# Forgetting attention, prompt part: when the maximum matmuls of later query blocks are issued

## The chip, the cores and the metric

The kernel is one launch on one core of a Trainium2 chip. It computes one inference step of a hybrid decoder layer. The metric is the device time of the core in microseconds (us), median of several executions. The engines are called PE (TensorE, with PEld for its weight loads), DVE (VectorE), ACT (ScalarE), POOL (GpSimd) and SP (SyncE, which issues DMAs).

## The reference

Only the attention over the prompt matters here: 8 heads of 64 channels, 4096 positions, causal, with a bias of cumulated forget logarithms.

```python
s = jnp.einsum('bqhd,bkhd->bhqk', q, k, preferred_element_type=jnp.float32) * ATTN_SCALE
s = s + (jnp.transpose(fq, (0, 2, 1))[..., :, None] - jnp.transpose(fk, (0, 2, 1))[..., None, :])
mask = k_pos[None, :] <= q_pos[:, None]
s = jnp.where(mask[None, None], s, -jnp.inf)
p = jax.nn.softmax(s, axis=-1)
return jnp.einsum('bhqk,bkhd->bqhd', p.astype(v.dtype), v)
```

The rest of the layer (input projection, pooling mixer, attention over the paged cache for 32 sample tokens, gates, output projection) runs in other phases, before and after this one, and is not touched.

## The kernel before

The phases run one after the other; the change is in `phase_attend`. The queries of a head are cut into 8 blocks of 512, so there are 64 blocks `b`, with row `j` = 0 to 7 inside head `h`. Block `b` of row `j` is worked through in `j + 1` groups of 512 keys (288 groups `n` in all, 36 a head). The last group of each block holds the causal diagonal: it is called diagonal here, the others full. A group is two steps `s` (576 in all), a step is two halves, and a half is a tile of scores of 128 keys by 512 queries.

The softmax needs the maximum of every query before its block begins. It is found ahead of time in units: one unit is the matmul of 128 queries with 512 keys (L997, in the diagonal chunk narrower, 128, 256 or 384 columns, with one more matmul for the mask, L1000) into one of the two PSUM banks of `mx`, and a DVE reduction of that bank to one column (L928). A block of row `j` has 4 * (j + 1) units, 1152 in all. When all units of block `b + 1` are reduced, DVE combines them (L933, L938), PE spreads the result over a row (`spread_shift`, L1008, four matmuls into the same banks), and ACT copies it into `q_one` (L834); scores of block `b + 1` wait for that copy. A unit, a spread and a sum of weights (`total`, L1060) all take the next of the two banks, and PE waits in `bank_free` until the use before the last one has been read: for a unit, until its reduction is done.

The order of PE is written out by hand. For each step: scores of half 0 (L1028, L1029, and in a diagonal group L1032 for the mask), the first `len // 2` units of the step, scores of half 1, the remaining units. After the last step of a block comes the spread for the next block. After the two steps of a group come the matmuls of weights with values of the step before and of this group's first step (`weigh`, L1049), and in the second group of the next block the sums of weights of the previous one (`total`). PE runs in order, so a unit that waits for its bank holds back everything behind it.

How many units stand in which step is set by `units_by` (the number issued up to step `n`). DVE's order follows the same list: the units of a step, then `combine` in the last but one step of a block, `low_q` (L922) in its last, and `low_k` (L916) in step `first_step[b] + 4` of the blocks of rows 3 to 6 of heads 0 to 6 and of rows 1 and 2 of head 0. That step is the first one of the third group, counted from the block's start. `low_k` makes the low parts of the next head's keys, in 1024 columns, from two tiles in SBUF. POOL adds the weights in pairs (L802, L803) in the meantime, ACT computes the exponentials (L852, in diagonal groups L856).

```python
def units_after(n, half):
    units = units_in(n)
    return units[:len(units) // 2] if half == 0 else units[len(units) // 2:]
```

With `units_by` as it is, a step of the kernel before has two units almost everywhere, and 3 in 22 steps of head 0, where the lead over the running block is built up; the last 17 steps have none.

Of the kernel before, what the change touches and what calls it, by code (L numbers as in the profile page):

```python
# [10 lines left out]

# [1 line left out]

# [21 lines left out]
NT = SEQ // TILE  # L37
TT = TILE // P
# [529 lines left out]
def phase_attend(nc, io, keep):  # L568

    NB = H * NT  # L570
# [3 lines left out]
    EARLY = 3 * TT  # L574
# [10 lines left out]
    def row(b):  # L585
        return b % NT

    quad_base = [sum(row(a) + 1 for a in range(b)) for b in range(NB + 1)]
    NQUAD = quad_base[NB]
    NSTEP = 2 * NQUAD  # L590
    block_of = [b for b in range(NB) for _ in range(row(b) + 1)]
    first_step = [2 * quad_base[b] for b in range(NB)]
    last_step = [2 * quad_base[b + 1] - 1 for b in range(NB)]
    unit_base = [TT * quad_base[b] for b in range(NB + 1)]

    units_by = [0] * NSTEP
    for n in reversed(range(NSTEP)):
        b = block_of[n // 2]
        needed = unit_base[min(b + (2 if n >= last_step[b] - 1 else 1), NB)]
        units_by[n] = max(needed, units_by[n + 1] - 3 if n + 1 < NSTEP else 0)  # L600
    out = EARLY
    for n in range(NSTEP):
        out = units_by[n] = min(max(out + 2, units_by[n]), unit_base[NB])

    def units_in(n):
        return range(units_by[n - 1] if n else EARLY, units_by[n])
# [1413 lines left out]
def build(nc, io):  # L2020
    with ExitStack() as ctx:
        m = Alloc(nc, ctx, "keep")
        keep = {
            "ident": m.sb("ident", [P, P]),
            "ones": m.sb("ones", [P, P]),
            "hs_high": m.sb("hs_high", [P, KC, NS], F32R),
            "hs_low": m.sb("hs_low", [P, KC, NS], F32R),
            "f_tot": m.sb("f_tot", [H, NT]),
        }
        phase_project(nc, io, keep)  # L2030
        phase_decode(nc, io, keep)
        phase_attend(nc, io, keep)
        keep["mix_s"] = m.sb("mix_s", [NS, D])
        phase_gates(nc, io, keep)
        phase_merge(nc, io, keep)
# [34 lines left out]
```

## Time and profile before

| what | us |
| --- | --- |
| median of 3 runs | 3806.81 |
| lowest, highest | 3802.3, 3811.97 |
| profiled execution | 3809.71 |
| its span | 3808.1 |
| prompt attention, first scores to last weigh, in that execution | 1179.4 to 2722.5 |

The profile is of one execution. Times in the rows are counted from the start of its span. "Idle" in brackets is the time that the engine stood still before an instruction, and the name behind the arrow is what ended it. PE rows show a matmul from its start to its modelled end; the next may start before that, so starts are what to compare. The granted clock is a share: 1.00 is 2.4 GHz, 0.50 is 1.2 GHz, and a value between is a mean over a stretch.

### The profile page before, as it was taken

To read this page: it belongs to the slowest core of one execution; us is meant where nothing else is said; L and a number is where in the kernel's file an instruction comes from. 1 tells how busy PE (TensorE), PEld (TensorE's weight loads), DVE (VectorE), ACT (ScalarE), POOL (GpSimd) and SP (SyncE) were. 2 spreads that over 40 slices of the span, in tenths; PEclk is the share of its full clock that TensorE was granted. 3 is DMA by queue.
4 is the path that set the end of the run, shared out by engine and by line. 5 is a ranking of instruction groups with operands and counts; after the bars stand their busy time and mean duration, and the time that the engine had idled before them with its cause. 6 is when DMAs were issued, how large, how long until landed. Compare 5 with 4: busy or idle time off the path is not lost. (4 is left out here: it accounts for less than half of the span.)

```text
span 3808.1 us, 52765 instructions
## 1 busy us (share of the span) xinstructions
PE 3488.4 (92%) x18932; PEld 2413.4 (63%) x18932; DVE 1710.7 (45%) x2708; ACT 1174.9 (31%) x1611; POOL 1196.8 (31%) x1146
## 2 busy tenths in 40 slices
PE   7999999796966999999999999999799999978998
PEld 5777777672814555656565656565367777757887
DVE  3222221251516556555655555555244353445554
ACT  4221221040314445454545454554410000000110
POOL 0000000133333566666666666666500000000000
PEclk9999999796977999999999999999899999989999
DMA  4222332399884121212121212100212111136765
GB/s 147 96 93 102 119 110 78 137 353 353 295 323 99 25 45 34 45 34 45 34 45 34 46 34 45 34 17 12 85 54 77 44 44 55 55 101 186 207 212 163
DMA packets 215996, 392.36 MB, mean 103 GB/s; under 512 B 60135, under 2 KB 102120, under 8 KB 213775
## 3 DMA queue, kind: packets, MB, share of 16 engines
q1 hardware_dynamic: 195079, 322.22, 27.2%
q0 software_dynamic: 20768, 68.17, 4.8%
q8 instruction: 92, 1.51, 0.2%
q14 instruction: 57, 0.47, 0.0%
HBM read 288.50 MB, written 101.99 MB: 103 GB/s over the span
## 5 line engine op out<-in xcount | busy, mean ns | idle before, releaser
L928 DVE TENSOR_REDUCE at_max_parts<-at_mx 128x1 f32<-128x512 f32 (+3 forms) x1152 | 731.4, 646 | 498.3 <-PE at_mx L997 428.9
L802 POOL TENSOR_TENSOR at_pair_sum<-at_probs 128x1024 f32<-128x1024 f32 x224 | 532.0, 2375 | 428.5 <-ACT at_probs L852 428.5
L852 ACT ACTIVATE at_probs<-at_st,at_gap 128x1024 f32<-128x1024 f32 x448 | 497.5, 1112 | 526.9 <-PE at_st L1029 525.9
L1049 PE MATMUL at_o_ps<-at_probs,at_v 128*64 128x512 f32 (+3 forms) x2304 | 544.9, 584 | 0.0
L1028 PE MATMUL at_st<-at_q_all,at_k_all 128*128 128x512 f32 (+3 forms) x1152 | 477.4, 414 | 0.0
L997 PE MATMUL at_mx<-at_k_one,at_q_top 67*128 67x512 f32 (+3 forms) x1152 | 454.0, 395 | 8.7 <-DVE at_max_parts L928 5.9
L1029 PE MATMUL at_st<-at_q_one,at_k_one 67*128 67x512 f32 (+3 forms) x1152 | 439.6, 382 | 0.0
L1028 PEld LDWEIGHTS at_st<-at_q_all,at_k_all 128*128 128x128 f32 x1152 | 218.5, 190 | 225.9 <-ACT at_probs L852 108.7
L93 PE MATMUL ga_acc<-ga_h_high,ga_w_high 128*128 128x512 f32 x768 | 312.3, 407 | 22.5 <-DVE ga_h_low L1293 21.0
L94 PE MATMUL ga_acc<-ga_h_low,ga_w_high 128*128 128x512 f32 x768 | 308.7, 402 | 0.0
L95 PE MATMUL ga_acc<-ga_h_high,ga_w_low 128*128 128x512 f32 x768 | 308.4, 402 | 0.0
L803 POOL TENSOR_TENSOR at_quad_sum<-at_pair_sum 128x512 f32<-128x512 f32 x224 | 287.5, 1284 | 17.5
L1049 PEld LDWEIGHTS at_o_ps<-at_probs,at_v 128*64 128x64 f32 x2304 | 146.8, 138 | 209.2 <-issue 159.4
L997 PEld LDWEIGHTS at_mx<-at_k_one,at_q_top 67*128 67x128 f32 x1152 | 220.2, 191 | 64.6 <-DVE at_max_parts L928 17.1
L1029 PEld LDWEIGHTS at_st<-at_q_one,at_k_one 67*128 67x128 f32 x1152 | 221.2, 192 | 30.1
L93 PE MATMUL mg_acc<-mg_w_high,mg_mix_high 128*128 128x512 f32 x512 | 201.5, 394 | 24.1 <-DVE mg_xs L1598 16.9
L93 PE MATMUL pj_acc<-pj_h_high,pj_w_high 128*128 128x512 f32 x512 | 209.9, 410 | 6.3 <-DVE pj_fs L430 6.3
L1522 POOL MEMSET mg_minus_half<- 128x1 f32 x1 | 0.1, 98 | 656.7 <-POOLq L66 656.7
L95 PE MATMUL pj_acc<-pj_h_high,pj_w_low 128*128 128x512 f32 x512 | 206.1, 403 | 0.0
L94 PE MATMUL pj_acc<-pj_h_low,pj_w_high 128*128 128x512 f32 x512 | 205.8, 402 | 0.0
L94 PE MATMUL mg_acc<-mg_w_low,mg_mix_high 128*128 128x512 f32 x512 | 200.7, 392 | 0.0
L95 PE MATMUL mg_acc<-mg_w_high,mg_mix_low 128*128 128x512 f32 x512 | 200.5, 392 | 0.0
(302 smaller groups left out, 4974.5 us busy)
## 6 DMA issues: line engine op xcount, KB each, us to landing
dc_pages<-in_cache_k_dram SPq DMA_DIRECT2D x128, 256.0 KB, 6.0
dc_pages<-in_cache_k_dram POOLq DMA_DIRECT2D x128, 256.0 KB, 5.7
dc_pages<-in_cache_v_dram SPq DMA_DIRECT2D x128, 256.0 KB, 7.1
dc_pages<-in_cache_v_dram POOLq DMA_DIRECT2D x128, 256.0 KB, 5.7
pj_x<-in_x_prompt_dram SPq DMA_DIRECT2D x32, 512.0 KB, 3.7
scratch_h_t<-pj_h_t SPq DMA_DIRECT2D x8, 2048.0 KB, 9.9
at_q_raw<-scratch_q_t SPq DMA_DIRECT2D x128, 128.0 KB, 3.0
at_k_raw<-scratch_k_t SPq DMA_DIRECT2D x64, 256.0 KB, 4.1
```

The lines of the kernel that those rows point to most:

```text
L93: nc.tensor.matmul(out, lhs_high, rhs_high, start=first, stop=False)
L94: nc.tensor.matmul(out, lhs_high, rhs_low, start=False, stop=False)
L95: return nc.tensor.matmul(out, lhs_low, rhs_high, start=False, stop=last)
L802: chain.link(nc.gpsimd.tensor_tensor(pair, first, second, ALU.add))
L803: nc.gpsimd.tensor_tensor(out, pair[:, 0], pair[:, 1], ALU.add).then_inc(summed, 1)
L852: nc.scalar.activation(probs[:, s % RING], st[:, s % 2], ACT.Exp, bias=bias).then_inc(exp_done, 1)
L928: nc.vector.tensor_reduce(max_parts[:, b % AHEAD, t, c:c + 1], mx[:, bank_of["unit", k] % 2, 0:width], AX_X, ALU.max).then_inc(bank_done, 1)
L997: last = nc.tensor.matmul(mx[:, n % 2, 0:width], q_top[0:KR, b % AHEAD, t * P:(t + 1) * P], k_one[h % 2][0:KR, c * TILE:c * TILE + width], ...
L1028: nc.tensor.matmul(out, k_all[h % 2][:, keys], q_all[:, b % AHEAD, at:TILE], start=True, stop=False)
L1029: last = nc.tensor.matmul(out, k_one[h % 2][0:KR, keys], q_one[0:KR, b % 2, at:TILE], start=False, stop=(c < j))
L1049: last = nc.tensor.matmul(o_ps[half * HD:(half + 1) * HD, b % 2, at:TILE], v[:, h % 2, 4 * c + own], probs[:, s % RING, half, at:TILE], st ...
L1522: nc.gpsimd.memset(minus_half[:], -0.5)
```

## The change

Only `units_by` is computed differently: a step of a diagonal group gets at most one unit, a first step of a full group two and a second step three, from the second head on; in head 0 every step may have three. A floating line (`even`, `lead`) spreads them over the blocks so that each block's units are still issued in time. The number of units, their order, the banks and all other instructions stay as they are.

```diff
-    units_by = [0] * NSTEP
-    for n in reversed(range(NSTEP)):
-        b = block_of[n // 2]
-        needed = unit_base[min(b + (2 if n >= last_step[b] - 1 else 1), NB)]
-        units_by[n] = max(needed, units_by[n + 1] - 3 if n + 1 < NSTEP else 0)
-    out = EARLY
+    def on_diagonal(n):
+        return n // 2 + 1 == quad_base[block_of[n // 2] + 1]
+
+    def most_units(n):
+        return 3 if n < 2 * quad_base[NT] else 1 if on_diagonal(n) else 2 + n % 2
+
+    finished_by = [unit_base[min(block_of[n // 2] + (2 if n >= last_step[block_of[n // 2]] - 1 else 1), NB)] for n in range(NSTEP)]
+    needed = list(finished_by)
+    for n in reversed(range(NSTEP - 1)):
+        needed[n] = max(needed[n], needed[n + 1] - most_units(n + 1))
+    per_head = TT * quad_base[NT] - 2 * NT
+    even = list(itertools.accumulate(1 if on_diagonal(n) else per_head / (2 * (quad_base[NT] - NT)) for n in range(NSTEP)))
+    lead = max(f - e for f, e in zip(finished_by, even))
+    units_by, out = [], EARLY
     for n in range(NSTEP):
-        out = units_by[n] = min(max(out + 2, units_by[n]), unit_base[NB])
+        out = max(needed[n], out, min(out + most_units(n), math.floor(lead + even[n] + 0.01), unit_base[NB]))
+        units_by.append(out)
```

Worked through, the two formulas give these counts of groups by the units of their two steps; "with low_k" are those whose first step has a `low_k` behind its units:

| group | before | after |
| --- | --- | --- |
| full, 2 and 2 | 206 | 90 |
| full, 2 and 3 | 6 | 115, of these 25 with low_k |
| full, 3 and 2 | 0 | 6, of these 2 with low_k |
| full, 3 and 3 | 5 | 6, of these 2 with low_k |
| full, none | 7 | 7 |
| diagonal, 2 and 2 | 56 | 0 |
| diagonal, 3 and 2 | 6 | 0 |
| diagonal, 1 and 1 | 0 | 58 |
| diagonal, 3 and 3, or 3 and 1 | 0 | 3 |
| diagonal, others (2 and 0, 1 and 0, none) | 2 | 2 |

In heads 1 to 6 a head then has 8 diagonal groups with 1 and 1, 12 full ones with 2 and 3 that have no `low_k`, 4 with 2 and 3 that have one (the third group of rows 3 to 6; the third unit of row 3's is 128 wide), and 12 with 2 and 2. Head 7 has no `low_k`.

## Rows read from the trace of the kernel before

**Rows 1.** The page: its first lines.
```profile
span 3808.1 us, 52765 instructions
PE 3488.4 (92%) x18932; PEld 2413.4 (63%) x18932; DVE 1710.7 (45%) x2708; ACT 1174.9 (31%) x1611; POOL 1196.8 (31%) x1146
```

**Rows 2.** Waits of the whole run: engine, line, releaser: us in total, times, longest.
```profile
PE at_mx L1008 <- DVE at_max_parts L928: 39.6, 54, 2.0
```

**Rows 3.** By stretch: A:B us, then busy us of PE, PEld, DVE, ACT, POOL, granted clock, DMA share, GB/s. Four full groups.
```profile
1714.37:1719.23 4.86, 4.86 (x22) 2.67 (x20) 2.77 (x4) 2.23 (x2) 3.66 (x3) 1.00 0.00 0
1292.76:1298.20 5.44, 5.36 (x24) 2.85 (x22) 3.36 (x5) 2.23 (x2) 4.30 (x3) 1.00 0.00 0
1709.48:1714.37 4.89, 4.89 (x25) 2.73 (x21) 3.87 (x6) 2.23 (x2) 2.76 (x3) 1.00 0.00 0
1256.48:1263.12 6.64, 5.36 (x26) 2.89 (x22) 4.80 (x7) 2.23 (x2) 4.91 (x4) 1.00 0.25 68
```

**Rows 4.** Timeline, DVE in the full group at 1714.37: start, us, instruction, count, idle.
```profile
1715.39 2.78 DVE L928 TENSOR_REDUCE at_max_parts<-at_mx 128x1 f32<-128x512 f32 x4 [1.25 <-PE at_mx L997]
```

**Rows 5.** The view by source line: ns shortest/median/longest of the reductions and of low_k.
```profile
L928 DVE TENSOR_REDUCE at_max_parts<-at_mx x1152: 280/692/695, 1169.6 to 2685.8; 128x1 f32<-128x512 f32 x168, 128x1 f32<-128x128 f32 x16, 128x1 f32<-128x384 f32 x8
...
L916 DVE TENSOR_TENSOR at_k_all<-at_k_raw,at_k_all x32: 1221/1222/1461, 1168.3 to 2475.3; 64x1024 fp32r<-64x1024 f32 x32
```

**Rows 6.** Timeline, the two units at the end of the group at 1292.76.
```profile
1295.42 0.98 PE L997 MATMUL at_mx<-at_k_one,at_q_top 67*128 67x512 f32 x2
```

**Rows 7.** Timeline, the full group with low_k and five units at 1256.48.
```profile
1257.67 1.29 POOL L803 TENSOR_TENSOR at_quad_sum<-at_pair_sum 128x512 f32<-128x512 f32 x1
...
1258.59 1.46 DVE L916 TENSOR_TENSOR at_k_all<-at_k_raw,at_k_all 64x1024 fp32r<-64x1024 f32 x1
...
1260.08 1.98 DVE L928 TENSOR_REDUCE at_max_parts<-at_mx 128x1 f32<-128x512 f32 x3
...
1260.83 0.50 PE L997 MATMUL at_mx<-at_k_one,at_q_top 67*128 67x512 f32 x1 [1.28 <-DVE at_max_parts L928]
```

**Rows 8.** By stretch, as rows 3: diagonal groups of rows 0, 1, 2, 5, 6; then row 4.
```profile
1776.55:1781.87 5.32, 4.92 (x31) 3.41 (x30) 3.27 (x7) 3.56 (x8) 1.42 (x3) 1.00 0.01 3
1788.29:1793.99 5.70, 5.63 (x42) 3.47 (x38) 3.40 (x8) 2.47 (x5) 3.57 (x5) 1.00 0.49 126
1803.82:1809.63 5.81, 5.33 (x33) 3.38 (x29) 4.27 (x8) 2.47 (x5) 4.45 (x5) 1.00 0.44 121
...
1882.31:1888.47 6.16, 5.27 (x31) 3.28 (x29) 4.12 (x7) 2.48 (x5) 5.35 (x6) 1.00 0.00 0
1918.74:1924.50 5.76, 5.28 (x33) 3.53 (x31) 3.16 (x7) 2.48 (x5) 4.95 (x5) 1.00 0.00 1
...
1468.37:1476.12 7.75, 6.88 (x32) 3.80 (x30) 3.68 (x7) 2.48 (x5) 5.58 (x6) 0.78 0.00 0
```

**Rows 9.** Timeline, the diagonal group at 1882.31 (2 and 2 units, row 5).
```profile
1882.95 0.45 PE L997 MATMUL at_mx<-at_k_one,at_q_top 67*128 67x512 f32 x1
...
1883.23 0.34 PE L1028 MATMUL at_st<-at_q_all,at_k_all 128*128 128x384 f32 x1
...
1883.43 1.39 DVE L928 TENSOR_REDUCE at_max_parts<-at_mx 128x1 f32<-128x512 f32 x2 [2.19 <-PE at_mx L997]
...
1883.64 0.45 PE L997 MATMUL at_mx<-at_k_one,at_q_top 67*128 67x512 f32 x1
...
1886.25 0.42 PE L1008 MATMUL at_mx<-at_ident_r,at_shift_w 128*65 128x128 f32 x4 [0.89 <-DVE at_max_parts L928]
1886.61 0.20 PEld L1049 LDWEIGHTS at_o_ps<-at_probs,at_v 128*64 128x64 f32 x4
```

**Rows 10.** Timeline, the diagonal group at 2683.98, whose last step has no unit.
```profile
2685.09 1.45 DVE L928 TENSOR_REDUCE at_max_parts<-at_mx 128x1 f32<-128x512 f32 x2 [2.18 <-PE at_mx L997]
...
2686.57 0.36 DVE L933 TENSOR_TENSOR at_max_moved<-at_max_parts,at_gap 128x32 f32<-128x32 f32 x1
...
2687.22 0.46 PE L1008 MATMUL at_mx<-at_ident_r,at_shift_w 128*65 128x128 f32 x4 [0.71 <-DVE at_shift_w L938]
```

More of the change, by code:

```diff
@@ L14 @@
+import itertools
+import math
 from contextlib import ExitStack
```

## The prediction, made before the change was run

> **What bounds the kernel now.** I read the page first: PE is busy for 92% of the span, and DVE, ACT and POOL for less than half of it [rows 1]. The change moves matmuls and reductions inside the prompt attention, which is 1543 us of the span, so I left the page for that stretch and cut it into groups, each from the first L1028 of one group to the first of the next. A full group with four units takes 4.86 us and PE is busy through all of it [rows 3]; there PE's own work sets the time. DVE reduces the four units in 2.78 us without a gap between them [rows 4]: one reduction of 512 columns takes 0.69 us, the median [rows 5], and PE brings a new unit just as often (two score matmuls and one unit). So DVE is half idle over the group, but while the units run it has no slack at all, and with two banks a unit can start only when the reduction before the last one has ended. A diagonal group of rows 3, 4, 5 and 7 takes 6.1 us though its scores are narrower, and PE is busy for 5.27 us of it [rows 8]: PE brings units faster than DVE reduces them, and the spread at the end stands still for 0.89 us until a reduction has freed its bank [rows 9]. Over the run that wait is met 54 times and costs 39.6 us of idle PE [rows 2]. That is what the change can take away. What it adds lands in full groups, where PE never waits now.
>
> **The diagonal groups.** Two units leave each of them. The first that is left stands after the second half of the first step. Where two are there now, the second starts 1.33 us into the group (1883.64 less 1882.31), and the one before it holds 0.28 us of that (1883.23 less 1882.95) [rows 9], so the new one starts at 1.05. Its reduction starts 0.48 us later (1882.95 to 1883.43) [rows 9]. What follows is seen in the one group whose last step has no unit: two reductions take 1.45 us there, so the second begins at about 2685.85, the combine starts at 2686.57 and the spread at 2687.22, now released by the combine [rows 10]: 1.37 us from reduction to spread. So the spread starts at 1.05 + 0.48 + 1.37 = 2.90. PE gets to it at about 2.2 (narrow scores and one more unit), so some 0.7 us of idle stays, by another releaser. From spread to weigh it is 0.36 us and from there to the next group 1.86, up to the group's end [rows 8, 9]: 5.12 us. The low_q and the reduction behind the combine lie beside the 1.86 us of weigh and cost nothing; the exponentials too. Against the groups of now [rows 8] this gives, for rows 0 to 7, 0.20, 0.58, 0.69, 1.04, 1.04, 1.04, 0.64 and 1.04: 6.27 us a head, and 43 us for heads 1 to 7 (seven times, less the last group, which has no units at all). Bounds: 0.1 us either way for each of 55 groups, so 37 to 49.
>
> Six of the diagonal groups of heads 1 to 7 take 7.60 to 7.80 us in place of 6.1. One is shown: its mean granted clock is 0.78, so for a part of it PE ran at 1.2 GHz, behind that same wait [rows 8]. With the idle time before the spread cut and fewer narrow matmuls around it, I take these away: 6 times 1.6, 9.6 us. Bounds 0 and 9.6.
>
> **The fifth unit in a full group.** In heads 1 to 7 there are 84 full groups with 2 and 3 units and no low_k. Head 0 already has two of them with full width, and both took 5.44 us; one is shown [rows 3]. Of the extra 0.58 us about 0.23 is the matmul itself; the rest is pacing: the last two units stand one behind the other, the fifth has to wait for the third's reduction, and PE's next work, the weigh, is behind it in order. The pair spans 0.98 us where a single unit spans 0.40 [rows 6]. 84 times 0.58 is 48.7 us. Below, only the matmul would be left, 19 us; above, nothing in the trace is dearer for this shape, and I allow 0.65, 55 us.
>
> **The fifth unit behind low_k.** In 24 groups of heads 1 to 6 the copy of the keys' low parts stands on DVE between the second unit and the third. With four units it is free: 4.89 us, the third row [rows 3], since the fourth unit's bank needs only the second's reduction. With five it is not. The one such group of head 0 with full widths took 6.64 us, the fourth row [rows 3]: low_k from 1258.59 to 1260.05, the third unit's reduction after it, and PE idle for 1.28 us until that has ended, with the fifth unit and the whole weigh behind it [rows 7]. That is 1.75 us over the four-unit group. In row 3 the third unit is 128 wide, its reduction 0.28 in place of 0.69 [rows 5], so 1.34 there. Per head 3 * 1.75 + 1.34 = 6.59, and for six heads 39.5 us. Bounds: the plain price, 0.58 each, 14 us, and 1.29 us more each (below), 70 us.
>
> What shows in low_k's own row is that it isn't always 1.22 us long: 1.46 where POOL's L803 runs beside its start, until 1258.96 [rows 5, 7]. The Trainium skill, "SBUF — State Buffer", under "SBUF: two separate sides", has a rule for this: a DVE operation with two SBUF inputs and a GpSimd one that reads SBUF exclude each other, and the one that comes second blocks for the whole instruction. By that rule low_k would be held by whatever add of POOL it meets; the trace agrees in direction (1.46 against 1.22), but in its own duration it shows 0.24 us, not a whole add. As a mechanism of this kernel it is a rival below.
>
> These groups are also new places where PE stands still for over a microsecond, longer than before the spreads. The group of rows 7 kept its clock at 1.00 [rows 3]. I put 2 or 3 of 24 at 1.6 us each for a lowered clock, 4 us; bounds 0 and 38.
>
> **Head 0.** It gets ten more steps with three units (32 against 22), at 0.58 us some 6 us, and about 2 us more behind its low_k, and loses as much at four diagonal groups that come down to one and one. I take it as zero, within 8 us.
>
> **Sum.** Of the profiled execution, 3809.7: + 48.7 + 39.5 - 43 - 9.6 + 4 + 0 = + 39.6, so 3849.3. The median of the runs shown is 2.9 us under the profiled execution, so 3846 for the median.
>
> **The rivals.**
> First, the clock: PE's waits behind low_k bring it down to 1.2 GHz in half or all of the 24 groups, as it came down in six diagonal groups of now. For it: those six had only about 0.9 us of idle. Against it: those had narrow matmuls around the wait, and the group of rows 7, with 1.28 us, had none of it. 12 to 24 times 1.6 less the 4 above: 3861 to 3880. Chance 0.08.
>
> Second, the lock: in the new rhythm low_k meets POOL's adds at another point and is held for a whole L803 of 1.29 us [rows 7]. 24 times up to 1.29, 31 us more: up to 3877. That is where the page's rule would lead. Against it: full groups get longer, so POOL has more time and its add should end before low_k comes, not after. If so, low_k falls from 1.46 to 1.22, which gives back up to 6 us. Chance 0.06 for over 3868.
>
> Third, low_k falls out of the way (ready so early or so late that the third reduction isn't behind it): the 24 groups cost 0.58 each, the sum falls by 25 us to 3821. For it: only one row carries the price. Against it: DVE's order is written out, low_k always stands before the third unit. Chance 0.10, half of it within 0.3%.
>
> Fourth, not slower: the fifth unit costs its matmul only, because the reduction that it waits for ends in time. Then 108 fifths at 0.23 cost 25 us against 52.6 saved, and the kernel would be at 3779. It decides where the mean price of the 108 falls below 52.6 / 108 = 0.49 us; the rows have 0.58 and 1.75. Against it: four reductions in 2.78 us with no gap [rows 4] leave none for a unit that comes after 0.23. Chance 0.05.
>
> Fifth, the change does nothing that lasts: what diagonal groups give equals what full ones take, because the banks only move the wait. That would need the low_k groups near the plain price and the clock's 9.6 us full; it gives 3800 to 3818. Chance 0.06.
>
> **How the numbers follow.** The forecast, 3825 to 3860 with 3846 as its middle, has 0.65. The range of 8 in 10, 3822 to 3866, adds the near half of the first and the third rival; what lies above (the clock and the lock at full size) and below (fourth and fifth) is left out. A measurement of this kernel can tell about 0.3%, 11 us, from no change. Slower by over that: the forecast, the first two and half of the third rival, and what is left over near them, 0.87. Within it: the other half of the third and most of the fifth, 0.08. Faster: 0.05.
>
> **What would show it.** In the profile after: diagonal groups of one and one unit at 5.0 to 5.2 us, the spread released by the combine (L938) and no longer by L928; full groups of 2 and 3 at 5.4, with PE idle before the second unit of the last pair; the third groups of rows 3 to 6 in heads 1 to 6 at 6.2 to 6.7, with over a microsecond of idle released by L928; heads 1 to 6 each some 6 us longer, head 7 about 1 us. The wait of L997 for L928 takes the place of L1008's. The prediction is wrong if full groups with five units come in under 5.1 us, or if the low_k groups don't stand out.

## The result and the profile after

| | median us | lowest, highest | ratio to before, 95% interval |
| --- | --- | --- | --- |
| kernel before | 3806.24 | 3802.3, 3811.97 | |
| changed kernel | 3871.49 | 3865.56, 3872.18 | 1.0167 [1.0149, 1.0184] |

The changed kernel is slower by 65 us. The forecast was 3846, its range 3822 to 3866. The sign and the mechanism were right, the size was not. The profiled execution took 3872.18 us, 62.5 us more than the one of before, where the forecast had 39.6. The ratios here and below are those of the fast runs made beside each other, without one execution of the kernel before that took 4614.52 us at a lower clock, so they differ by up to 0.1% from the quotient of two medians.

In the changed kernel the line numbers are 11 higher: the unit is L1008, its mask L1011, its reduction L939, low_k L927, the combine L944 and L949, the spread L1019, scores L1039 and L1040, weigh L1060, POOL's adds L813 and L814. The counts and times by group below are of the one profiled execution of each kernel.

The page: every engine has as many instructions as before, and PE's busy time is longer by 42 us all the same (to be held against rows 1).

```profile
span 3870.6 us, 52765 instructions
PE 3530.9 (91%) x18932; PEld 2408.9 (62%) x18932; DVE 1697.4 (44%) x2708; ACT 1174.5 (30%) x1611; POOL 1195.1 (31%) x1146
```

The waits of the changed kernel (engine, line, releaser: us in total, times, longest). The spread hardly waits for a bank any more (0.9 us, where it was 39.6 before [rows 2]) but for the combine, 19.8 us in all, and the units now wait for the reductions:

```profile
PE at_mx L1008 <- DVE at_max_parts L939: 39.7, 32, 1.5
PE at_mx L1019 <- DVE at_shift_w L949: 19.8, 40, 1.2
PE at_mx L1019 <- DVE at_max_parts L939: 0.9, 2, 0.5
```

Stretches of the changed kernel, with the columns of rows 3 (us, busy us of PE, PEld, DVE, ACT, POOL, granted clock, DMA share, GB/s): a plain full group with five units; a five-unit group with low_k whose clock stayed up, and one whose clock fell; diagonal groups of rows 5 and 7; then head 0, and heads 1 to 7.

```profile
1989.47:1994.91 5.44, 5.30 (x24) 3.04 (x23) 3.14 (x5) 2.23 (x2) 3.72 (x3) 1.00 0.00 0
1895.83:1902.56 6.73, 5.37 (x26) 2.86 (x22) 4.87 (x7) 2.23 (x2) 4.79 (x4) 1.00 0.00 0
1866.00:1873.96 7.96, 6.59 (x27) 3.08 (x23) 4.88 (x7) 2.23 (x2) 5.96 (x4) 0.85 0.26 67
1913.08:1918.56 5.48, 4.71 (x28) 2.82 (x26) 3.28 (x5) 2.37 (x5) 5.10 (x5) 1.00 0.02 3
1994.91:1999.76 4.85, 4.72 (x29) 2.83 (x27) 2.17 (x5) 2.37 (x5) 3.96 (x4) 1.00 0.00 0
...
1179.20:1399.10 219.90, 209.34 (x1068) 120.50 (x1066) 124.74 (x206) 104.81 (x131) 123.03 (x86) 0.92 0.14 32
1399.10:2783.00 1383.90, 1326.84 (x7680) 777.23 (x7679) 727.86 (x1217) 691.20 (x877) 871.10 (x617) 0.99 0.15 35
```

The same two stretches, head 0 and heads 1 to 7, of the kernel before:

```profile
1179.40:1393.90 214.50, 203.89 (x1066) 118.75 (x1064) 126.39 (x205) 104.31 (x131) 124.81 (x88) 0.95 0.14 33
1393.90:2722.50 1328.60, 1293.46 (x7681) 780.86 (x7680) 739.38 (x1218) 691.88 (x877) 871.04 (x614) 0.99 0.16 36
```

The rest of the span differs by less than 2 us. Cutting both traces into their 288 groups, each from the first score matmul of one to that of the next, and adding up by kind gives where the time went:

| kind (heads 1 to 7 unless said) | groups | before | after | difference | forecast |
| --- | --- | --- | --- | --- | --- |
| diagonal | 56 | 337.5 | 283.5 | -54.0 | -52.6 |
| full, five units, no low_k | 84 | 404.7 | 451.8 | +47.1 | +48.7 |
| full, five units, low_k | 24 | 118.0 | 176.9 | +58.9 | +43.5 |
| full, others | 88 | 468.4 | 471.7 | +3.3 | 0 |
| head 0 | 36 | 214.5 | 219.9 | +5.4 | 0 |

The third row of the table stands out. In this trace 12 of the 24 groups had a stretch at 1.2 GHz, as the third row of the fence above; the other twelve took 6.46 us (row 3) or 6.72. This is the wait, in the group at 1895.83, with the columns of rows 7: low_k between the second and the third reduction, and PE idle for 1.36 us before the fifth unit, until the third's reduction had ended.

```profile
1896.83 1.39 DVE L939 TENSOR_REDUCE at_max_parts<-at_mx 128x1 f32<-128x512 f32 x2 [0.57 <-PE at_mx L1008]
...
1898.26 1.22 DVE L927 TENSOR_TENSOR at_k_all<-at_k_raw,at_k_all 64x1024 fp32r<-64x1024 f32 x1
...
1899.51 1.98 DVE L939 TENSOR_REDUCE at_max_parts<-at_mx 128x1 f32<-128x512 f32 x3
...
1900.26 0.50 PE L1008 MATMUL at_mx<-at_k_one,at_q_top 67*128 67x512 f32 x1 [1.36 <-DVE at_max_parts L939]
```

### The profile page after: what moved, and what is told of

The parts are those of the page before. It is cut to its first block and busy times, and to the rows that moved or that the text cites. A ratio compares the mean times of both kernels' runs of the same rounds, so it can differ in the third digit from the quotient of the medians.

```text
span 3870.6 us, 52765 instructions
## 1 busy us (share of the span) xinstructions
PE 3530.9 (91%) x18932; PEld 2408.9 (62%) x18932; DVE 1697.4 (44%) x2708; ACT 1174.5 (30%) x1611; POOL 1195.1 (31%) x1146
## 5 line engine op out<-in xcount | busy, mean ns | idle before, releaser
L939 DVE TENSOR_REDUCE at_max_parts<-at_mx 128x1 f32<-128x512 f32 (+3 forms) x1152 | 730.2, 646 | 576.6 <-PE at_mx L1008 401.9
L813 POOL TENSOR_TENSOR at_pair_sum<-at_probs 128x1024 f32<-128x1024 f32 x224 | 530.5, 2368 | 499.8 <-ACT at_probs L863 499.8
L1060 PE MATMUL at_o_ps<-at_probs,at_v 128*64 128x512 f32 (+3 forms) x2304 | 552.5, 591 | 0.0
L1008 PE MATMUL at_mx<-at_k_one,at_q_top 67*128 67x512 f32 (+3 forms) x1152 | 456.4, 400 | 49.6 <-DVE at_max_parts L939 39.7
L1039 PE MATMUL at_st<-at_q_all,at_k_all 128*128 128x512 f32 (+3 forms) x1152 | 485.1, 421 | 0.4
L1040 PE MATMUL at_st<-at_q_one,at_k_one 67*128 67x512 f32 (+3 forms) x1152 | 441.2, 383 | 0.0
L1039 PEld LDWEIGHTS at_st<-at_q_all,at_k_all 128*128 128x128 f32 x1152 | 219.1, 190 | 232.9 <-issue 157.5
L95 PE MATMUL ga_acc<-ga_h_high,ga_w_high 128*128 128x512 f32 x768 | 311.8, 406 | 23.2 <-DVE ga_h_low L1304 21.0
L1008 PEld LDWEIGHTS at_mx<-at_k_one,at_q_top 67*128 67x128 f32 x1152 | 221.4, 192 | 144.2 <-DVE at_max_parts L939 99.6
L814 POOL TENSOR_TENSOR at_quad_sum<-at_pair_sum 128x512 f32<-128x512 f32 x224 | 287.2, 1282 | 17.6
L1060 PEld LDWEIGHTS at_o_ps<-at_probs,at_v 128*64 128x64 f32 x2304 | 148.0, 139 | 207.6 <-issue 167.8
L1040 PEld LDWEIGHTS at_st<-at_q_one,at_k_one 67*128 67x128 f32 x1152 | 222.0, 193 | 24.9
```

The lines of the kernel that those rows point to most:

```text
L95: nc.tensor.matmul(out, lhs_high, rhs_high, start=first, stop=False)
L813: chain.link(nc.gpsimd.tensor_tensor(pair, first, second, ALU.add))
L814: nc.gpsimd.tensor_tensor(out, pair[:, 0], pair[:, 1], ALU.add).then_inc(summed, 1)
L939: nc.vector.tensor_reduce(max_parts[:, b % AHEAD, t, c:c + 1], mx[:, bank_of["unit", k] % 2, 0:width], AX_X, ALU.max).then_inc(bank_done, 1)
L1008: last = nc.tensor.matmul(mx[:, n % 2, 0:width], q_top[0:KR, b % AHEAD, t * P:(t + 1) * P], k_one[h % 2][0:KR, c * TILE:c * TILE + width], ...
L1039: nc.tensor.matmul(out, k_all[h % 2][:, keys], q_all[:, b % AHEAD, at:TILE], start=True, stop=False)
```

## The experiments

Ten kernels. All but the fifth start from the changed one. A fence has the line numbers of its own kernel.

**1. low_k behind the units of its group.**

```diff
-    low_k_at = {s + 1: c for s, (c, part) in round_k_at.items() if part == 1}
+    low_k_at = {s + 2: c for s, (c, part) in round_k_at.items() if part == 1}
```

> The changed kernel with one edit: low_k stands one step later on DVE, behind the third, fourth and fifth unit of the third group and not between the second and the third. Units, PE's order and diagonal groups stay. Theory (the 24 groups of heads 1 to 6 with five units and low_k, 7.37 us on average in the changed kernel, carry both the wait of PE for the third reduction and the clock that falls behind it): they come down to the price of a plain five-unit group, about 5.4 us, 24 * 1.95 = 46 us less, so 3871 - 46 = 3825, and the granted clock stays at 1.00 in nearly all of heads 1 to 6. Rival 1 (the clock falls for another reason, for instance the five-unit groups themselves): only the wait goes, some 28 us, so 3843, and about a dozen dips of the clock stay. Rival 2 (low_k only moves its wait to the next group): 3871, with L997 idle for L939 in the fourth group.

Measured: 3841.74 us, 1.0092 [1.0074, 1.0111] of before. The 24 groups came down from 7.37 to 5.37 us on average and none had a lowered clock, as the theory said; that is 48 us, where 46 were expected. But the next full group of the block took 5.96 us in place of 5.23, and heads 1 to 7 had three dips of the clock at other places (in the diagonal groups behind row 3's low_k), so the whole came to 3842 and not to 3825. The timeline shows why, the second rival by a cause of its own: low_k now runs beside POOL's pair addition.

```profile
1857.31 2.36 POOL L813 TENSOR_TENSOR at_pair_sum<-at_probs 128x1024 f32<-128x1024 f32 x1 [1.65 <-ACT at_probs L863]
...
1857.71 3.04 DVE L927 TENSOR_TENSOR at_k_all<-at_k_raw,at_k_all 64x1024 fp32r<-64x1024 f32 x1
...
1859.75 2.13 POOL L814 TENSOR_TENSOR at_quad_sum<-at_pair_sum 128x512 f32<-128x512 f32 x1
...
1861.53 0.50 PE L1008 MATMUL at_mx<-at_k_one,at_q_top 67*128 67x512 f32 x1 [0.65 <-DVE at_max_parts L939]
```

low_k takes 3.04 us, against 1.22 in the fence above, and POOL's second addition 2.13 against 1.29 [rows 7]. The starts say more: low_k ends 1.08 us after POOL's first addition (1860.75 against 1859.67), and POOL's second addition ends 1.13 us after low_k (1861.88). Each ends as if it had done next to nothing until the other was through.

**2. The same with POOL's additions left out beside low_k.** The groups with low_k are missing from the sums of weights here.

```diff
+                if n + 1 < quad_base[b + 1] and any(x in low_k_at for x in (2 * n, 2 * n + 1)):
+                    chain.link(nc.gpsimd.memset(out, 1.0))
+                    nc.gpsimd.memset(out[:, 0:1], 1.0).then_inc(summed, 1)
+                    return
```

> The changed kernel with low_k one step later, and in the groups with low_k POOL leaves out the two additions of the weights and writes ones, so the sums of weights lack these groups. In the run with low_k late, low_k took 3.08 us in the median where it takes 1.22 alone, and the fourth group of the block, 4.9 us in the changed kernel, took 5.8. Theory (DVE's low_k and POOL's addition of the same time exclude each other at SBUF): low_k is back at 1.22 us and the fourth groups at 4.9 and 5.5, 22 groups times 1 us and a few dips of the clock behind them: 3842 - 22 - 6 = 3814. Rival (low_k is long there for a reason of its own, such as the reductions around it): still 3 us, 3842.

Measured: 3813.0 us, 1.0006 [0.9997, 1.0016]. low_k is back at its own time. First its row in the view by source line (shortest/median/longest in ns) from the first experiment, then from this one, where it is L931:

```profile
L927 DVE TENSOR_TENSOR at_k_all<-at_k_raw,at_k_all x32: 1221/3084/3232, 1169.9 to 2507.2; 64x1024 fp32r<-64x1024 f32 x32
```

```profile
L931 DVE TENSOR_TENSOR at_k_all<-at_k_raw,at_k_all x32: 1222/1222/1637, 1169.6 to 2478.1; 64x1024 fp32r<-64x1024 f32 x32
```

The groups behind low_k fell to 5.07 us, and no clock fell in heads 1 to 7. So low_k and POOL's addition hold each other up. The rule of the Trainium skill that the prediction set beside this ("SBUF — State Buffer", "SBUF: two separate sides") was right in full size. The rows of the kernel before had shown it already: low_k met only the last 0.37 us of L803 there, and ended 1.09 us after it (1260.05 less 1258.96 [rows 7]), as here 1.08. The prediction took the 0.24 us of extra duration for the size of the effect, when it was the size of the overlap that was small.

**3. low_k in two halves.** The second half one step later.

```diff
                     if s in low_k_at:
-                        low_k(low_k_at[s])
+                        low_k(low_k_at[s], 0)
+                    if s - 1 in low_k_at:
+                        low_k(low_k_at[s - 1], 1)
```

> The changed kernel with low_k cut into two instructions of 512 columns: the first where low_k stood, the second one step later. The same work, but the third reduction is held back by some 0.6 us in place of 1.2. Theory (the clock falls because of the length of PE's wait): the wait of the 24 groups shrinks from about 1.3 to 0.7 us, 3 * 0.6 + 0.5 a head, 14 us less over six heads, and the dips of the clock go too, up to 17 us more: 3840. Rival (the dips do not depend on the length of this wait): 3857, with about a dozen dips left in heads 1 to 6.

Measured: 3832.87 us, 1.0068 [1.0046, 1.0091]. The wait was 0.81 us (its row is below, beside that of the next run), the 24 groups took 6.12 us on average, and there was no dip in heads 1 to 7: of the 30 us that they lost, 13 are the wait and 17 the clock. (The second half met POOL's addition here and took up to 2.79 us in place of 0.69, but nothing waited for it.)

**4. low_k's work twice.** First into a spare tile, then as before.

```diff
+                nc.vector.tensor_tensor(spare[HD:P], k_raw[HD:P, n % 2], low.bitcast(F32), ALU.subtract)
                 nc.vector.tensor_tensor(low, k_raw[HD:P, n % 2], low.bitcast(F32), ALU.subtract).then_inc(k_low, 1)
```

> The changed kernel with the work of low_k done twice, the first time into a spare tile: the third reduction of the low_k groups is held back by some 2.4 us in place of 1.2. It is the other side of the run with low_k in halves (wait of 0.7 us, no dip of the clock in heads 1 to 6; in the changed kernel, with 1.3, about twelve in 24 groups). Theory (the clock falls by the length of PE's wait): the 24 groups are 1.2 us longer each by the wait, 29 us, with 3 more in head 0, and nearly all of them now have a dip, ten or more further ones at up to 1.7 us: 3871 + 32 + 17 = 3920. Rival (dips are not set by the wait's length): 3903, and no more dips than in the changed kernel.

Measured: 3941.78 us, 1.0347 [1.0327, 1.0366]. The wait was 2.50 us, and 21 of the 24 groups had a lowered clock, 9.23 us on average. That is 22 us more than expected, by the clock: the time at 1.2 GHz in the whole prompt attention went from 74.5 to 157.9 us, and half of the difference is 42 us, where 17 were put down. The row of the fifth unit with halves, and then with the work twice (L1016 and L1010 there):

```profile
1878.96 0.49 PE L1016 MATMUL at_mx<-at_k_one,at_q_top 67*128 67x512 f32 x1 [0.81 <-DVE at_max_parts L945]
```

```profile
1903.58 0.80 PE L1010 MATMUL at_mx<-at_k_one,at_q_top 67*128 67x512 f32 x1 [2.50 <-DVE at_max_parts L941]
```

With the changed kernel between them this is a series: waits of 0.81, 1.36 and 2.50 us (in row 3 some 0.25 us less) in otherwise equal groups, and a lowered clock in 0, 12 and 21 of 24. Over all of heads 1 to 7 the time at 1.2 GHz was 0, 41 and 113 us. Here are heads 1 to 7 of these two runs in the view by stretch, granted clock third from the end; the changed kernel's row, with 0.99, is above.

```profile
1393.60:2744.80 1351.20, 1307.74 (x7680) 772.83 (x7679) 759.95 (x1241) 691.26 (x877) 879.37 (x616) 1.00 0.16 36
```

```profile
1414.10:2854.10 1440.00, 1355.68 (x7680) 789.33 (x7679) 755.17 (x1241) 691.30 (x877) 885.98 (x616) 0.96 0.15 33
```

The length of the wait is not all of it. In the changed kernel the clock fell in 6 of 6 groups of row 4 (wait 1.37 us), 4 of 6 of row 5 (1.36), 2 of 6 of row 3 (1.12), and in none of row 6, whose wait is the longest. One of these last, by stretch and in the timeline:

```profile
1929.82:1936.55 6.73, 5.32 (x27) 3.04 (x23) 4.61 (x7) 2.23 (x2) 4.55 (x4) 1.00 0.01 2
```

```profile
1934.25 0.50 PE L1008 MATMUL at_mx<-at_k_one,at_q_top 67*128 67x512 f32 x1 [1.41 <-DVE at_max_parts L939]
```

So the three kernels show that a longer wait lowers the clock more often; what decides it for a single group stays open.

**5. The kernel before, with one weigh ahead of the spread.** No unit is moved.

```diff
                     if s == last_step[b] and b + 1 < NB:
+                        if n >= 1:
+                            weigh(2 * n - 1)
                         spread_shift(b + 1)
-                if n >= 1:
+                if n >= 1 and not (n + 1 == quad_base[b + 1] and b + 1 < NB):
                     weigh(2 * n - 1)
```

> The kernel before (two units in nearly every step) with one edit on PE: in the last group of a block the weigh of the step before is issued ahead of the spread for the next block and not behind it. Theory (what diagonal groups lose is the wait of the spread for a bank or for the combine, not the units as such): the wait of about 0.9 us lies beside 0.93 us of weigh; some 5.3 us a head, 40 us in all, and the ten dips of the clock behind that wait, up to 16 us more: 3750 to 3766, without moving a single unit. Rival (DVE bounds the diagonal group, so PE only waits somewhere else): 3806.

Measured: 3764.8 us, 0.9889 [0.9873, 0.9906] of before. The group that stood at 1882.31 [rows 8], with the same four units, takes 5.39 us, and the spread (L1008 here, L928 the reduction) has no idle time before it:

```profile
1865.98:1871.37 5.39, 5.39 (x31) 3.20 (x29) 4.12 (x7) 2.48 (x5) 4.65 (x5) 1.00 0.00 0
```

```profile
1869.09 1.28 DVE L928 TENSOR_REDUCE at_max_parts<-at_mx 128x1 f32<-128x512 f32 x2
...
1869.97 0.46 PE L1008 MATMUL at_mx<-at_ident_r,at_shift_w 128*65 128x128 f32 x4
```

**6. The fifth unit between the two weighs** of its group, on PE only.

```diff
                     weigh(2 * n - 1)
+                for k in held:
+                    unit(k)
                 weigh(2 * n)
```

> The changed kernel with one edit on PE: the last of three units in the second step of a full group is issued between the two weighs, about 0.93 us later; low_k stays where it is. Theory (in a plain five-unit group 0.35 of the 0.58 us is the wait for the third unit's reduction): the 84 plain groups of heads 1 to 7 fall from 5.38 to about 5.05 us, 29 us less; in the 24 low_k groups the wait shrinks from about 1.3 to 0.6 us, 16 us less, and if the clock follows the wait up to 17 us more: 3809 to 3826. Rival (a fifth unit costs 0.58 us wherever it stands, because PE's own work grows by that): no change, 3871.

Measured: 3826.96 us, 1.0049 [1.0031, 1.0068]. Half of it held: the low_k groups fell to 5.82 us and no clock fell in heads 1 to 7. The plain groups stayed where they were (5.39 us, 5.38 in the changed kernel), as the rival had it: the unit no longer waits, but from it to the next weigh it is 0.44 us, where a unit beside scores costs 0.23.

```profile
1972.67 1.08 PE L1060 MATMUL at_o_ps<-at_probs,at_v 128*64 128x512 f32 x4
...
1973.68 0.51 PE L1008 MATMUL at_mx<-at_k_one,at_q_top 67*128 67x512 f32 x1
...
1974.12 1.08 PE L1060 MATMUL at_o_ps<-at_probs,at_v 128*64 128x512 f32 x4
```

**7. The fifth unit behind both weighs,** so beside the next group's scores, low_k in its old place. The same lines, with `weigh(2 * n)` ahead of the loop over `held`.

> The changed kernel with one edit on PE: the last of three units in the second step of a full group is issued behind both weighs, not behind the scores and not between the weighs; low_k stays where it was, between the second and the third unit. The run with the unit between the weighs left the plain groups at 5.38 us. Theory (that was PE's price of changing from the weigh's form of matmul to another and back, which is saved where a unit stands beside scores; the third reduction, over at 4.3 us into a low_k group, no longer holds anything): plain five-unit groups at 5.1 us, 84 * 0.3 = 25 us less than in the changed kernel, low_k groups at about 5.15 in place of 7.37, 53 us less, head 0 some 5 less: 3788. Rival (a fifth unit costs 0.5 us on PE wherever it stands): 3871 - 24 * 2 - 5 = 3818.

Measured: 3785.26 us, 0.9930 [0.9913, 0.9948]. A plain group and one with low_k:

```profile
1945.43:1950.50 5.07, 5.07 (x24) 3.09 (x24) 2.75 (x5) 2.23 (x2) 3.65 (x3) 1.00 0.00 0
1856.52:1861.72 5.20, 5.20 (x25) 2.97 (x22) 4.19 (x6) 2.23 (x2) 3.30 (x3) 1.00 0.00 0
```

PE is busy through both, and the expectation of 3788 held. The low_k groups fell from 7.37 to 5.20 us on average, 52 us, with low_k unchanged in place and size: by itself it costs next to nothing (plain groups take 5.13), only the fifth unit that had to be on time behind it did.

**8. Runs 7 and 5 together,** on the changed kernel.

> The run before with one more edit: in the last group of a block the first weigh stands ahead of the spread. Theory (both orders of units then keep PE busy without a wait, and the units moved out of diagonal groups cost in full groups what they saved): diagonal groups at 4.8 us, 14 us under the run before, so 3774, no faster than the kernel before with the weigh first (3765). Rival (moving units is still worth something once nothing waits): under 3755.

Measured: 3762.67 us, 0.9873 [0.9856, 0.9889]; the interval of experiment 5 overlaps it. It was expected at 3774; its diagonal groups fell to 4.77 us from 5.12 in experiment 7, more than the 0.25 allowed for. Heads 1 to 7 of this kernel, then of experiment 5:

```profile
1387.90:2676.00 1288.10, 1288.05 (x7680) 765.85 (x7679) 748.82 (x1218) 687.83 (x877) 872.25 (x616) 1.00 0.16 37
```

```profile
1391.60:2681.20 1289.60, 1289.60 (x7681) 771.87 (x7680) 739.38 (x1219) 691.94 (x877) 872.12 (x616) 1.00 0.16 37
```

In both PE is busy from end to end, and it makes 1.5 us in 1289 whether the units stand in diagonal groups or not.

**9 and 10. Two combinations that missed.** Experiments 1 and 6 together, and these two with the edit of experiment 5.

> Both edits of the two runs before it together, on the changed kernel. Theory: every fifth unit costs its matmul alone, 0.23 us; 84 * 0.35 = 29 and 24 * (7.37 - 5.1) = 54 us go, so 3788, which is under the kernel before (3806), since the diagonal groups' gain of some 53 us is then paid for with only 108 * 0.23 = 25 us. Rival (moving units out of diagonal groups is worth nothing in itself): 3806 or more.

Measured: 3847.57 us, 1.0100 [1.0078, 1.0123].

> The changed kernel with three edits: low_k one step later, the fifth unit between the two weighs, and in the last group of a block the first weigh ahead of the spread. Theory: to the 3788 expected of the first two comes the 0.7 us wait of the spread for the combine in 60 diagonal groups, some 39 us: 3749, the same as the kernel before with the weigh first, since both are then bound by the same PE work. Rival (the spread is late for the next block's first scores once the group is shorter): 3770 or more, with PE idle at L1028 for ACT's copy in q_one.

Measured: 3825.1 us, 1.0045 [1.0028, 1.0062]. They were expected at 3788 and 3749. Both expectations count on a late low_k costing nothing and on 29 us from the fifth unit between the weighs. Neither is so: the groups behind low_k took 5.99 us in both, by the collision of experiment 1, and the plain five-unit groups took 5.45 us, no less than in experiments 1 and 6. That the first of the two is even slower than experiment 1 alone (5.8 us) goes with head 0, whose time at 1.2 GHz was 40.1 us against 23.2 there, 27 us of it in its diagonal groups against 11; half of 16.9 is 8.4 us. Between the two kernels the edit of experiment 5 gave 22 us, 21.7 of them in the diagonal groups of heads 1 to 7, and not the 39 that were expected. Those took 0.7 us for each of 60 spreads, but in the changed kernel the wait for the combine is 19.8 us in all (the row further above), and some of the 22 is the clock's, whose time at 1.2 GHz fell from 46.9 to 33.7 us.

## Why the prediction fell short, point by point

**The diagonal groups: right in the sum, not row by row.** -54.0 against -52.6 us, clock included: no diagonal group of heads 1 to 7 had a lowered clock any more. But the flat 5.12 us stands for groups of 4.56 us (row 0) to 5.48 (rows 4 and 5), and that the sum is met so closely is in part luck. The wait of 0.7 us before the spread, released by the combine, is there in rows 4 and 5 alone (0.75 to 0.77); in the others it is 0 to 0.32 us in nearly every group. What sets these two apart is seen in row 5, where POOL's addition and the combine's first instruction (two tiles of SBUF, like low_k) meet:

```profile
1914.72 1.27 POOL L814 TENSOR_TENSOR at_quad_sum<-at_pair_sum 128x512 f32<-128x512 f32 x1
...
1915.38 0.66 DVE L944 TENSOR_TENSOR at_max_moved<-at_max_parts,at_gap 128x28 f32<-128x28 f32 x1
...
1916.32 0.46 PE L1019 MATMUL at_mx<-at_ident_r,at_shift_w 128*65 128x128 f32 x4 [0.77 <-DVE at_shift_w L949]
```

L944 ends 0.05 us after POOL's addition here (1916.04 against 1915.99). It is as short as 0.16 us where it meets none, and so is the same instruction of the kernel before, where the median was 0.38 us (shortest/median/longest in ns, the kernel before first):

```profile
L933 DVE TENSOR_TENSOR at_max_moved<-at_max_parts,at_gap x64: 156/378/860, 1172.1 to 2686.6; 128x4 f32<-128x4 f32 x8, 128x8 f32<-128x8 f32 x8, 128x12 f32<-128x12 f32 x8, 128x16 f32<-128x16 f32 x8
```

```profile
L944 DVE TENSOR_TENSOR at_max_moved<-at_max_parts,at_gap x64: 157/182/773, 1171.9 to 2747.2; 128x4 f32<-128x4 f32 x8, 128x8 f32<-128x8 f32 x8, 128x12 f32<-128x12 f32 x8, 128x16 f32<-128x16 f32 x8
```

The 0.36 us of the combine in the prediction's 1.37 us from reduction to spread [rows 10] hold such a meeting too. That it is the same collision as in experiment 2 is read from these rows and was not tried by itself.

**The plain fifth unit: right.** +47.1 against +48.7. Of the 0.56 us of one, experiment 7 takes 0.25 away, the wait: it leaves 5.13 us on average of 5.38. The prediction had split it as 0.23 for the matmul and 0.35 for the wait, so the wait's part was put 0.1 us too high and the rest as much too low.

**The fifth unit behind low_k: wait right, clock wrong.** Without the time at 1.2 GHz the 24 groups cost 41.5 us (58.9 less half of 34.8), against 39.5.

**The clock: the step that failed.** The term "2 or 3 of 24 at 1.6 us each for a lowered clock, 4 us" was mis-sized. It was 12 of 24, which is 17 us in these groups, and 3 us in the groups behind them, into which it ran on: 20 us in place of 4. I had one group of that kind without a dip [rows 3, 7] and gave it more weight than the six dips behind waits of 0.9 us. The first rival, with a chance of 0.08, is what happened: half of the groups, for which it gave 3861. The 10 us up to the measured 3871 are mostly head 0's clock (5), the groups behind (3) and the time outside the attention (2). That the waits behind low_k bring the clock down is shown by experiments 4, 7 and 3: with the wait at 2.50, 0 and 0.81 us the clock fell in 21, 0 and 0 of the 24.

**Head 0: taken as zero, was +5.4.** Its time at 1.2 GHz went from 23.2 to 33.5 us, which at half speed is 5.1 of it. The rest cancelled as forecast. (Four of its diagonal groups have 3 and 3 units or 3 and 1; the table ahead of the prediction says three.)

All in all the prompt attention was at 1.2 GHz for 43.7 us before and for 74.5 after. Half of the difference, 15.4 us, is the clock's part; the forecast had -9.6 + 4 = -5.6. Without it the attention became 60.7 - 15.4 = 45.3 us longer, and the forecast without it was 48.7 + 39.5 - 43 = 45.2. That this is met to 0.1 us is luck in part: without the clock the plain fifth units came out 3.4 us lower than forecast and the diagonal groups 1, the low_k groups 2 us higher and the other full groups, put at nothing, 2. So of the 22.9 us by which the sum missed the profiled execution, 21 are the clock. The other two are outside the attention, where nothing was changed. The median missed by 25.

**The rivals.** The lock hardly lengthened low_k in the changed kernel (1.22 us in the median, at most 1.36, in row 3), so the second rival fell; its rule decided experiments 1 and 2 and the last two instead. The third and the fifth fell with the low_k groups at 6.46 us and more. The fourth, "the fifth unit costs its matmul only", is not what this change does, but it is nearly what experiment 7 does: the rival put such a kernel at 3779, and experiment 7 measured 3785, with 0.31 us for a fifth unit where the rival had 0.23.

## What to carry to other kernels

A unit of work that is moved from a place where an engine waits into one where it doesn't is paid there in full, and more if its partner engine is paced without slack; look first for other work that can be put into the wait (here one weigh, 42 us, no unit moved). When a move creates the same wait in many places, price the lowered clock behind it from the share of such waits that have it in the trace, not from a single one, and expect more than that share where the new wait is longer. Here the share of the kernel before was 6 dips in 27 diagonal groups with waits of 0.86 to 0.99 us, which would have given 5 of 24; behind 1.36 us it was 12. Before moving an instruction of DVE with two SBUF inputs, look at what POOL does at its new time, and hold its end against the end of POOL's instruction, not only its duration against the usual one.

## What the runs showed of the hardware that was not expected

- A `tensor_tensor` of DVE with both inputs in SBUF and a `tensor_tensor` of POOL stretch each other: 1.22 to 3.04 us for the one and 1.29 to 2.13 us for the other. The first was back to a median of 1.22 when POOL's was taken away. Low_k ended 1.08 to 1.09 us after POOL's addition whether it had met 0.37 us of it (kernel before) or 1.96 (experiment 1). The Trainium skill, "SBUF — State Buffer", under "SBUF: two separate sides", has it as a lock held for the whole instruction; the 3.04 us, 1.96 us from low_k's start to the end of POOL's addition and 1.08 more, agree with that.
- PE's granted clock fell behind waits of about a microsecond in an else busy stretch: in 0, 12 and 21 of 24 groups for waits of 0.81, 1.36 and 2.50 us (one profiled execution each). Within one kernel it was 6 of 6 behind 1.37 us in row 4 and 0 of 6 behind 1.41 in row 6, so the length is not all that decides.
- A 512-column unit takes PE 0.23 us, from its start to the next one's, among score matmuls and 0.44 us between two weighs, whose matmuls are 128*64 (rows 128*64 of L1060 against 67*128 of L1008 in experiment 6). Why is not shown.
